# A sparse-expert decoder layer: h kept in DRAM during the experts, and ten result buffers in place of two

## The reference

```python
h = x + W_out(sigmoid(g_A) * (A @ U_A) + sigmoid(g_B) * (B @ U_B))
y = h + HierMoE(RMSNorm(h))     # top-1 of 4 groups, then top-2 of 8 experts

def _hier_moe(u, ...):
    ...                                      # router: combine[n, e], two experts for each token
    hg = jnp.einsum('nd,edf->nef', ut, w_gate_e)
    hu = jnp.einsum('nd,edf->nef', ut, w_up_e)
    hid = jax.nn.silu(hg) * hu * combine[..., None]
    return jnp.einsum('nef,efd->nd', hid, w_down_e)
```

## Time and profile before

| | us |
|---|---|
| median of 3 runs | 3710.12 |
| lowest, highest | 3707.89, 3710.62 |
| the profiled execution | 3709.48 |
| its span, first to last instruction | 3707.7 |

### The profile page before, as it was taken

One profiled execution on the slowest core, in us unless ns is written; L12 is line 12 of the kernel. 1 busy time (PEld: TensorE's weight loads), 2 busy tenths in 40 slices (PEclk: granted clock), 3 DMA queues, 4 the chain that ended last, 5 costly groups with the idle time before them and its releaser, 6 DMA issues. The chain is left out here.

```text
span 3707.7 us, 32496 instructions
## 1 busy us (share of the span) xinstructions
PE 2900.2 (78%) x12555; PEld 1949.9 (53%) x12555; DVE 566.7 (15%) x1284; ACT 221.8 (6%) x537; POOL 68.3 (2%) x74
## 2 busy tenths in 40 slices
PE   8994999956658879888888887999998465565563
PEld 7883777745446747757567465777733222222221
DVE  0001001643321120111111211000001201101101
ACT  0001001201210000000000000000000000000000
POOL 0000000000000000000000000000000100000000
PEclk9997999965556576565665767999999677787776
DMA  5435332230035444444453442333333687686775
GB/s 187 136 91 195 121 118 102 91 150 1 0 118 193 133 156 158 137 159 137 152 171 128 153 153 91 124 116 123 124 114 110 273 338 301 252 340 267 287 305 214
DMA packets 153669, 604.16 MB, mean 163 GB/s; under 512 B 23081, under 2 KB 55986, under 8 KB 115954
## 3 DMA queue, kind: packets, MB, share of 16 engines
q1 hardware_dynamic: 137074, 554.87, 41.5%
q0 software_dynamic: 9200, 31.89, 2.4%
q10 hardware_dynamic: 7312, 16.25, 1.2%
HBM read 698.46 MB, written 34.36 MB: 198 GB/s over the span
## 5 line engine op out<-in xcount | busy, mean ns | idle before, releaser
L1061 PE MATMUL bank<-zt,arena 128*128 x2688 | 564.9, 365 | 15.8 <-DMA arena<-in_fox_k 15.8
L1061 PEld LDWEIGHTS bank<-zt,arena 128*128 128x128 f32 x2688 | 562.2, 326 | 18.9 <-issue 16.6
L1081 PE MATMUL bank<-arena,ut 128*64 128x512 f32 (+1 forms) x832 | 341.5, 578 | 52.6 <-ACT ut L1104 52.6
L423 PE MATMUL bank<-ut,wring 128*128 128x320 f32 x1408 | 381.7, 433 | 0.0
L423 PEld LDWEIGHTS bank<-ut,wring 128*128 128x128 f32 x1408 | 266.8, 190 | 110.1 <-issue 0.7
L1251 PE MATMUL bank<-ut,wring 128*128 128x320 f32 x1024 | 281.1, 435 | 10.1 <-DMA ut<-u_kept 10.1
L1081 PEld LDWEIGHTS bank<-arena,ut 128*64 128x64 f32 x832 | 129.0, 159 | 252.2 <-issue 181.9
L1251 PEld LDWEIGHTS bank<-ut,wring 128*128 128x128 f32 x1024 | 196.0, 192 | 92.4 <-DMA ut<-u_kept 10.3
L1775 PE MATMUL bank<-cst,arena 128*128 128x128 f32 x208 | 45.2, 389 | 188.9 <-DVE arena L1876 151.6
L1825 PE MATMUL bank<-wdn,par 128*32 128x512 f32 x512 | 86.6, 809 | 115.3 <-DVE par L1890 86.4
L1775 PEld LDWEIGHTS bank<-cst,arena 128*128 128x128 f32 x208 | 35.9, 202 | 208.3 <-DVE arena L1876 155.5
(11 more groups left out here) (346 smaller groups left out, 2015.5 us busy)
## 6 DMA issues: line engine op xcount, KB each, us to landing
wgu<-in_w_gu SPq DMA_DIRECT2D x128, 1024.0 KB, 12.7
wring<-in_w_merge SPq DMA_DIRECT2D x64, 1024.0 KB, 4.9
arena<-in_fox_k SPq DMA_DIRECT2D x128, 512.0 KB, 4.1
arena<-in_fox_v SPq DMA_DIRECT2D x128, 512.0 KB, 3.4
wdn<-in_w_dn SPq DMA_DIRECT2D x32, 2048.0 KB, 23.9
wring<-in_w_proj SPq DMA_DIRECT2D x44, 1024.0 KB, 4.9
arena<-in_cmp_kv SPq DMA_DIRECT2D x64, 256.0 KB, 3.0
zt<-in_cmp_kv SPq DMA_DIRECT2D x64, 256.0 KB, 3.0
```

Of the source, the lines that this page charges most:

```text
L423: last = nc.tensor.matmul(m.bank[:, 2 + s % 2, 0:T], m.wring[:, s, k * P:(k + 1) * P], m.ut[:, k, :], start=(k == 0), stop=(k == KD - 1))
L1061: last = nc.tensor.matmul(m.bank[:, SBANK[x] + bk, col:col + w], slot[:, j * P:(j + 1) * P], q, start=True, stop=True)
L1081: last = nc.tensor.matmul(m.bank[0:C, bk, 0:width], ss[:, buf, pg, :], slot[:, j * width:(j + 1) * width], start=(pg == 0), stop=False)
```

## The change

h is stored to a new DRAM tensor `h_kept` at the start of the route stage, by ScalarE, before the u_tok stores. During the experts its 5120 columns serve as ten result buffers of 512 (NY = 10), and `yt1` goes. Each buffer has its own semaphore. When the last gate/up matmul is done, SyncE loads h back into free room of `wgu` (columns 10240 to 15359 of it, behind the room of the gathers); the weighted sums and the y_tok store use it there.

```diff
+NY = 10
...
-        self.yt1 = sb("yt1", P, 512)
...
-        self.yt = [m.flat[:, 2 * DM + 512:2 * DM + 1024], self.yt1[:, :]]
+        self.yt = [m.flat[:, KD * T + 512 * s:KD * T + 512 * s + 512] for s in range(NY)]
...
             nc.scalar.activation(rs, rs, ACT.Sqrt, bias=m.eps[:, :], scale=1.0 / DM).then_inc(rs_ready, 1)
+            act.dma_start(a["h_kept"], m.flat[:, KD * T:2 * KD * T]).then_inc(un_out, 16)
             act.wait_ge(un_ready, 2)
...
-            act.wait_ge(un_out, 64)
+            act.wait_ge(un_out, 80)
...
+        hb = back[:, 5 * DM:5 * DM + KD * T]
+        hb01 = hb[:, 0:2 * DM].rearrange("p (b n) -> p b n", b=2)
+        h_in = sem("h_in")
...
+            sp.wait_ge(gu_done, NTILE)
+            sp.dma_start(hb, a["h_kept"]).then_inc(h_in, 16)
             sp.wait_ge(add_step, 6)
-            sp.dma_start(a["y_tok"], m.flat[:, KD * T:2 * KD * T]).then_inc(m.stores, 16)
+            sp.dma_start(a["y_tok"], hb).then_inc(m.stores, 16)
...
-            for s in range(2):
-                pool.wait_ge(y_free[s], 16 * (NTILE // 2))
+            for s in range(NY):
+                pool.wait_ge(y_free[s], 16 * ((NTILE - s + NY - 1) // NY))
...
-                        "t (j n) -> j t n", j=4), e.yt[j % 2]).then_inc(y_free[j % 2], 16)
+                        "t (j n) -> j t n", j=4), e.yt[j % NY]).then_inc(y_free[j % NY], 16)
...
-                    if j >= 2:
-                        dve.wait_ge(y_free[j % 2], 16 * (j // 2))
-                    nc.vector.tensor_copy(e.yt[j % 2], m.bank[:, 6 + j % 2, :]).then_inc(y_ready, 1)
+                    if j >= NY:
+                        dve.wait_ge(y_free[j % NY], 16 * (j // NY))
+                    nc.vector.tensor_copy(e.yt[j % NY], m.bank[:, 6 + j % 2, :]).then_inc(y_ready, 1)
+            dve.wait_ge(h_in, 16)
             dve.wait_ge(back_in, 96)
...
-                    nc.vector.scalar_tensor_tensor(out=m.h01[:, b, :], in0=got[b][j], scalar=w[:, b:b + 1],
-                                                   in1=m.h01[:, b, :], op0=ALU.mult, op1=ALU.add).then_inc(add_step, 1)
-                hv = m.h2[:, :, :].rearrange("p q n -> p (q n)")
+                    nc.vector.scalar_tensor_tensor(out=hb01[:, b, :], in0=got[b][j], scalar=w[:, b:b + 1],
+                                                   in1=hb01[:, b, :], op0=ALU.mult, op1=ALU.add).then_inc(add_step, 1)
+                hv = hb[:, 2 * DM:2 * DM + 1024]
...
+    a["h_kept"] = nc.dram_tensor("h_kept", (P, KD * T), FP32, kind="Internal").ap()
```

More of the change, by code:

```diff
@@ L1683, in experts_stage @@
         dn_done, y_ready, y_free, y_tail, back_in = (
-            sem("dn_done"), sem("y_ready"), [sem("y_free0"), sem("y_free1")], sem("y_tail"), sem("back_in"))
+            sem("dn_done"), sem("y_ready"), [sem(f"y_free{s}") for s in range(NY)], sem("y_tail"), sem("back_in"))
         add_step, gu_free = sem("add_step"), sem("gu_free")
```

## The result

The changed kernel takes 3598.56 us (median of 4 runs, 3595.98 to 3601.04) against 3710.37 for the kernel before in the same comparison: a ratio of 0.9699, 95% interval 0.9682 to 0.9716. It is 111.8 us faster. The forecast was 59.5 us faster with a range that ended at 3626, so the sign and the place were right and the size was half of what came. The span falls by 3707.7 - 3599.2 = 108.5 us.

The account below looks back on a forecast made before the run. Two-buffer store waits were taken to hide a bound of four DMA engines carrying all stores. Terms -82.5 + 18 + 5 = -59.5 us from 3709.5 gave 3650 us, range 3626 to 3684.

Parts of the forecast that it names:

- What bounds the kernel: Experts' stage: waits for two result buffers hold up PE; once gone, four DMA engines carrying all result stores are left.
- The first rival: Experts' stage: stores spread over all engines, or the four not always the same; 3535 us, chance 0.04.
- Point 1: Experts' stage, ten buffers for two: four engines never idle, 646 us of work, last store at 3588.5, -82.5 us.
- Point 2: Experts' stage: idle left on the four engines at thirteen turns between experts, +18 us, ends 0 and 42.
- Point 3: Experts' stage: stores queue deeper, VectorE may wait if ten buffers fill, but the four engines have work: 0.
- the fourth rival: Experts' stage: ScalarE stands at a store's issue while others are queued, pace stays today's, h traffic open; 3722 us, chance 0.06.
- Points 4 to 6: h store in route stage hidden, 0; h reload delays last store, +5 us; eight more GpSimd semaphore waits, 0.
- What would show it: Experts' stage signs: y_slot waits under 150 us, DMA share near 0.80, clock near 0.75, stage end near 3611.
- the signs of being wrong: DMA share above 0.9, y waits above 400 us with the same end, ScalarE issues of many us, stage beginning after 2945.
- The ends of the range: Low: the -82.5 us bound with nothing added, 3626; high: four engines idle 50 us and h load at 6.2, 3684.

Follow-up runs that it names:

- e8: The changed kernel with every result stored a second time, to a tensor that nothing reads: 3733.96 us, ratio 1.0060 to the kernel before.
- e4: The changed kernel with each result stored by four DMAs of 32 rows in place of one: 3516.45 us, ratio 0.9474 to the kernel before.
- e2: The changed kernel with three result buffers in place of ten, h still in memory: 3644.59 us, ratio 0.9815 to the kernel before.
- e3: The changed kernel with four result buffers in place of ten, h still in memory: 3602.28 us, ratio 0.9709 to the kernel before.
- e7: The changed kernel without the store and reload of h, so y is not the layer's result: 3593.68 us, ratio 0.9680 to the kernel before.
- e1: The changed kernel with two result buffers in place of ten, h still in memory: 3715.32 us, ratio 1.0008 to the kernel before.

## Why the prediction was right in kind and wrong in size

**What bounds the kernel: right.** The waits for two buffers were the cover over a second bound, and that bound is four DMA engines. The first rival (stores over all engines) fell by e8 and by the tail at a share of 0.26; in e4, where they are spread on purpose, the stage came to 540 us, and the rival's sum for it (3535) was 19 too high.

**Point 1, the bound of -82.5 us: this is the step that failed.** Its term for the work of the four engines, 646 us, was too large. It took the shares of the earlier trace rows for work that must be done one after the other: 137 us of stores to 3654 and 16 behind, with 0.104 us a packet from the earlier trace rows. A share is the time that packets are recorded as under way. The queues of the changed kernel, when several stores are queued and nothing else runs (3547 to 3561 us), then over the whole stretch (2940 to 3563 us):

```profile
q10 hardware_dynamic: 716, 1.42, 26.1%
```
```profile
q1 hardware_dynamic: 21744, 191.37, 74.2%
q10 hardware_dynamic: 6864, 13.63, 5.6%
q0 software_dynamic: 7200, 13.09, 5.5%
```

716 packets in 14 us on four engines are 14 x 4 / 716 = 0.078 us each, not 0.104. In the earlier trace rows nearly the same share moved only 77 GB/s, as its packets were recorded as longer; with stores queued it is 102 GB/s. A likely reason is that with two buffers few stores were queued there; no run shows why a packet's recorded time grows. e8 gives 0.079 for the same packet in the middle of weights. The second pair of rows shows the rest of it. Added up for the four engines, the shares of the changed kernel are 74.2% + 4 x 5.6% + 5.5% = 102.1% of 623 us, 636 us, and the last packet ends 621 us after 2940: so recorded times overlap, by 15 us if the four engines are never idle (point 2). The forecast's sum for the same work, with 6 us for h, was 646 + 6 = 652: 16 us more, nearly all of it stores (153 us, where the rows above give 4 x 5.6% of 623 = 140). 16 + 15 = 31 us, and 3588.5 + 6 for h - 31 = 3563.5 is where the last store landed (3563.05). By packets a microsecond the stores are only 1716 x 0.079 = 135 us. What the four engines lost before the change, in idle time and in slow stores, was thus some 110 us of 731 (731 less 621), and not 84 of 714.

**Point 2, +18 us of idle that stays: wrong, about 0.** No turn starves the four engines. In stretches of 2 us from 2940 on, the DMA share of the kernel before lies under 0.24 in 59 of 357 (to 3654), and in 40 of them under 0.10; that of the changed kernel never does in 303 (to 3546). This is one of its lowest, with a share that still is four engines' worth:

```profile
3282.00:3284.00 2.00, 1.53 (x12) 1.12 (x16) 0.16 (x1) 0.64 (x2) 0.00 (x0) 0.96 0.24 92
```

The bytes agree, by an estimate: weights, h and gathers (191.37 + 13.09 MB) at the 425 GB/s of the earlier trace rows are 481 us, and with 135 us of stores that is 616 of the 621 us, which leaves some 5 for idle time. Together the two errors are 31 + 18 = 49 of the 52 us by which the forecast missed the gain (111.8 against 59.5).

**Point 3, deeper queues cost nothing: right in the sum, wrong in the mechanism.** The queue does not take ten stores. How many packets are outstanding when a held-up issue ends can be counted. Up to 3233.22 us, 21 stores (2772 packets of q10) had been issued; the queues from 2940 to there and to the end of that issue at 3244.84:

```profile
q10 hardware_dynamic: 2403, 4.78, 4.2%
```
```profile
q10 hardware_dynamic: 2520, 5.01, 4.2%
```

2772 - 2403 = 369 packets are outstanding when it begins, 92 for each engine or 2.8 stores, and 252 when it ends, 63 for each or 1.9. The fifteen other issues of 7 to 18 us end, by the same count, with 60 to 74 for each engine. It is not a plain limit: four issues went through in 0.7 us or less with 84 to 102 outstanding, and the last two of the stage, when no weights are loaded any more, in 2.3 and 0.8 us with 129 and 132, almost four stores. What decides between them stays open. So the mechanism of the fourth rival is real: with three stores outstanding ScalarE mostly stands until about two are left. What it got wrong is the price. It supposed that the pace stays today's because two or three stores stood in the queue already; in fact only two could ever stand there, and the third and fourth bring 71 and 42 us (e2, e3). With four buffers the longest issue is 8.7 us and with ten 17.8, at the same time within the intervals: the four engines do not run dry, and the hold-up costs nothing.

**Points 4 to 6, the h traffic and the rest: right.** In the route stage 0; at the end +5 was forecast and about 5 measured (e7), with two buffers 3 (e1).

**What would show it.** VectorE's y waits fell below 150 (to 0); the stretch at a quarter of the share is there; but the DMA share was to be near 0.80 and is 0.86, the clock 0.75 and is 0.81, and the stage was to end near 3611 and ends at 3563. Of the signs of being wrong one came: ScalarE's issues were to stay short and are up to 17.8 us. PE's waits name a load of wgu for 10.3 us and wdn not at all, which leaves open what the 112.1 us of "issue" are. The ends of the range, 3626 and 3684, are 1 us off their own terms, which give 3627 and 3683; nothing hangs on that.

The rule of the Trainium skill that the prediction weighed ("DMA: Bandwidth & Descriptors", section "Why a DMA increments its semaphore by 16 and not by 1") holds in the parts that the runs can show: the split into DMAs whose slowest dimension is 32 took the quarter shares away, and a store has 132 packets, 128 rows and 4 more, where with four DMAs q10 has 10576 - 7456 = 3120 more over 52 tiles, 60 a tile, which is four times 16 in place of 4. No run tells which four engines they are.

## What to carry to other kernels

When a store's wait is long, look first at how wide the store is: a row of the queues in which only that store runs, at a quarter of the share, meant four of sixteen engines here, and another split of the same bytes (here 82 us with ten buffers, and 175 on the kernel before, with no more memory at all) may be worth more than deeper buffering, of which two buffers more than before held the whole gain. When you count a resource's work for a bound, take packets a microsecond from a stretch in which it is surely backlogged, and not the recorded share: here it put 0.104 us on a packet that took 0.078. And a wait that vanishes from one engine can come back in the issue of another, here at no cost: compare the rate of the resource behind both before you price either.

## What was not expected of the hardware

- A DMA issue on ScalarE can hold up the engine itself when several stores are outstanding: up to 17.8 us, and the sixteen issues of over 7 us ended when 60 to 74 packets for each of its four engines were left. SyncE's issues of weights in the same stage took under 1 us each.
- With all sixteen engines loaded the stage moved 409 GB/s for 530 us, reads and 2 KB stores mixed, at a share of 1.00.
- The same share of a quarter was 77 GB/s with one store after another and 102 with stores queued.
